# Operand rows 32 bytes further apart, second weight buffers 16 bytes later, in a float32r transformer chain on one core

## What is computed

```
hn = rmsnorm(h, norm_mix[0]);  q, k, v = split(hn @ w_qkv_a)
h  = h + stick_breaking(q, k, v) @ w_o_a
h  = h + (silu(n(h) @ w_gate) * (n(h) @ w_up)) @ w_down
...                              # layer two: rope, dilated attention, SwiGLU
mod = silu(c) @ w_ada + b_ada;   proj = modulated(h) @ w_in
y_a = (b * conv3(c_s * v_s)) @ w_short_out
y_b = silu(layer_norm(conv31(v_c * sigmoid(gl)) + b)) @ w_conf_out
x  = x + g1 * ((g_a * y_a + g_b * y_b) @ w_o);  x = x + g2 * swiglu(...)
```

## Time and profile before

| what | value |
|---|---|
| median of 2 runs | 2050.95 us (2049.29 to 2052.61) |
| profiled execution, first to last instruction | 2050.8 us |
| mean granted TensorE clock | 0.997 of full speed |
| PE (matmul) busy | 98% of the span |
| PEld (weight load) busy | 80% |
| DVE, ACT, POOL busy | 52%, 39%, 31% |

### The profile page before, as it was taken

How to read it: one execution, slowest core, us unless ns; L and a number is a source line. 1 busy time by engine, 2 the same in 40 slices (tenths; PEclk the granted TensorE clock), 3 DMA queues, 4 the chain that set the end, 5 groups by cost and what they waited for, 6 DMA issues and landing times.

```text
span 2050.8 us, 28727 instructions
## 1 busy us (share of the span) xinstructions
PE 2016.6 (98%) x9556; PEld 1645.1 (80%) x9556; DVE 1066.4 (52%) x1445; ACT 798.3 (39%) x1182; POOL 629.0 (31%) x416
## 2 busy tenths in 40 slices
PE   7999999999999999999999999999999999999997
PEld 5777788888887777788888888888888888888886
DVE  6666644343465666544343456699855552332324
ACT  5545443342253444454332354222227352222224
POOL 1111255341134333246341254444444031001013
PEclk9999999999999999999999999999999999999999
DMA  4122244443234344244443332233323323333333
GB/s 155 62 72 82 83 143 166 162 144 102 92 112 93 82 84 111 77 140 174 151 146 99 95 123 73 94 101 92 102 92 93 102 83 99 95 95 100 92 102 103
DMA packets 64036, 218.80 MB, mean 107 GB/s; under 512 B 7792, under 2 KB 9968, under 8 KB 63856
## 3 DMA queue, kind: packets, MB, share of 16 engines
q1 hardware_dynamic: 60912, 213.96, 32.8%
q0 software_dynamic: 3072, 4.20, 1.6%
HBM read 211.83 MB, written 2.10 MB: 104 GB/s over the span
## 4 chain that ended last, share of the span: by engine, by line
PE 92%; DVE 3%; issue 2%; ACT 1%; POOL 1%; DMA 1%; DVEq 0%; SPq 0%; ACTq 0%; POOLq 0%
PE G L1524 28%; PE G L1526 28%; PE G L1525 28%; PE Z L1648 2%; PE O L1666 2%; PE Z L1629 2%; PE Z L1524 1%; PE Z L1526 1%; PE Z L1525 1%; DVE ez L940 0%; DVE sp L923 0%; DMA raw<-stream 0%; DVE Z L1053 0%; PE O L1675 0%; DMA qkv<-tmp 0%
## 5 line engine op out<-in xcount | busy, mean ns | idle before, releaser
L375 ACT ACTIVATE wh<-raw 128x1024 fp32r<-128x1024 f32 x338 | 358.5, 1061 | 970.0 <-PE G L1526 957.5
L1524 PE MATMUL G<-xh,wh 128*128 128x512 f32 (+1 forms) x1616 | 634.0, 392 | 10.3 <-DVE xl L835 9.5
L1525 PE MATMUL G<-xl,wh 128*128 128x512 f32 (+1 forms) x1616 | 626.9, 388 | 0.0
L1526 PE MATMUL G<-xh,wl 128*128 128x512 f32 (+1 forms) x1616 | 626.9, 388 | 0.0
L806 DVE TENSOR_TENSOR wl<-raw,wh 128x1024 fp32r<-128x1024 f32 x277 | 385.5, 1392 | 180.8 <-ACT wh L375 177.6
L1524 PEld LDWEIGHTS G<-xh,wh 128*128 128x128 f32 x1616 | 304.0, 188 | 82.8 <-issue 15.0
L1524 PE MATMUL G<-yh,wh 128*128 128x512 f32 x904 | 352.1, 389 | 3.8 <-POOL yl L1420 2.1
L1526 PEld LDWEIGHTS G<-xh,wl 128*128 128x128 f32 x1616 | 303.9, 188 | 63.3
L1525 PEld LDWEIGHTS G<-xl,wh 128*128 128x128 f32 x1616 | 304.2, 188 | 61.6 <-issue 1.0
L1526 PE MATMUL G<-yh,wl 128*128 128x512 f32 x904 | 350.6, 388 | 0.0
L1525 PE MATMUL G<-yl,wh 128*128 128x512 f32 x904 | 350.5, 388 | 0.0
(11 more groups left out here) (245 smaller groups left out, 1970.5 us busy)
## 6 DMA issues: line engine op xcount, KB each, us to landing
raw<-stream SPq DMA_DIRECT2D x340, 512.0 KB, 3.5
araw<-ada_w SPq DMA_DIRECT2D x48, 512.0 KB, 4.3
fraw<-stream SPq DMA_DIRECT2D x8, 512.0 KB, 4.7
qkv<-tmp POOLq DMA_DIRECT2D x64, 64.0 KB, 4.0
h<-x_t SPq DMA_DIRECT2D x8, 256.0 KB, 6.8
out_t<-h SPq DMA_DIRECT2D x16, 128.0 KB, 1.8
con<-const_d SPq DMA_DIRECT2D x1, 1344.0 KB, 10.3
cs<-c_row SPq DMA_DIRECT2D x1, 512.0 KB, 4.2
```

Source lines behind the costliest of these rows:

```text
L375: eng.activation(wh[s][:, :, :], raw[s][:, :, :], ACT.Copy).then_inc(w_hi, 1)
L1524: eng.matmul(total, hi[:, k, :], src_h[:, k, cols], start=k == 0, stop=False)
L1525: eng.matmul(total, hi[:, k, :], src_l[:, k, cols], start=False, stop=False)
L1526: mm = eng.matmul(total, lo[:, k, :], src_h[:, k, cols], start=False, stop=k == kt - 1)
```

## The change

Only declarations change: no instruction is added, removed or put elsewhere, and the sizes of what is read and written stay.

```
+ROW_APART, HALF_LAP, STEP = 8, 0, 4
...
-        xh, xl = sb("xh", [P, KD, SEQ], F32R), sb("xl", [P, KD, SEQ], F32R)
-        yh, yl = sb("yh", [P, KD, SEQ], F32R), sb("yl", [P, KD, SEQ], F32R)
+        def rows(name, width, apart, skip=0):
+            t = sb(name, [P, skip + KD * (width + apart)], F32R)
+            return t[:, skip:].rearrange("p (k s) -> p k s", k=KD)[:, :, 0:width]
+
+        xh, xl = rows("xh", SEQ, ROW_APART), rows("xl", SEQ, ROW_APART)
+        yh, yl = rows("yh", SEQ, ROW_APART, HALF_LAP), rows("yl", SEQ, ROW_APART, HALF_LAP)
         raw = [sb(f"raw{s}", [P, KD, P]) for s in range(2)]
-        wh = [sb(f"wh{s}", [P, KD, P], F32R) for s in range(2)]
-        wl = [sb(f"wl{s}", [P, KD, P], F32R) for s in range(2)]
+        wh = [rows(f"wh{s}", P, 0, STEP * s) for s in range(2)]
+        wl = [rows(f"wl{s}", P, 0, STEP * s) for s in range(2)]
```

## The result

| | before | after |
|---|---|---|
| median of the runs, us | 2050.95 (2049.29 to 2052.61), 2 runs | 2086.03 (2084.65 to 2087.41), 2 runs |
| ratio | 1 | **1.017**, 95% interval 1.014 to 1.020 |
| profiled span, us | 2050.8 | 2085.5 |
| mean granted clock | 0.997 | 0.997 |

What follows compares the result with a forecast made beforehand. PE, busy 98% of the span with near-gapless matmuls, was taken as the bound. 3/4 of 7,800 full-width matmuls at -6.7 ns, the rest 0, gave 5.0 ns each, 39 us: 2050.8 - 39 = 2012 us; range 1975 to 2082.

Steps and rivals of the forecast that it cites:

- the 3/4 unknown relations: Full-width matmuls brought to weight-to-row placements the trace does not show; priced at -6.7 ns each, 39 us in sum.
- half the surplus: Gain assumed for unknown placements: 6.7 ns of the 13.3 ns by which each full-width matmul distance exceeds streaming 512 columns.
- the 256-column row: Trace passages of 256-column matmuls: 120.0 ns with `wh`, 113.8 ns with `fwh` 64 bytes apart; 6.2 ns better.
- The bound on the upper side: Most that an unknown placement was taken to cost a full-width matmul, +6.7 ns, from the nearest trace rows.
- relation 0: Weights and rows at equal places, counted modulo 128 bytes; said to remain for 1/8 of all matmuls, price 0.
- the matmuls that were counted at 64 bytes: 1/8 of all matmuls, with weights and rows 64 bytes apart modulo 128; between -6.2 and +6.7 ns, taken as 0.
- The two rows at 512 columns: Trace passages 64 bytes apart: `fwh`, 12 distances of 233.3 ns, and `x2h`/`x2l`, 9 of 228.9; worse by 6.7 and 2.3 ns.
- The second argument: For the -6.7 ns price: a relation changing with each row cannot settle into one bad rhythm for a whole product.
- The ceiling: Most that changing addresses could gain over all full-width matmuls: 7,800 x 13.3 ns = 104 us, giving 1947 us.
- price 0: DVE, ACT and POOL work beside PE, none over 3% of the chain; no new wait expected, so no time added.
- the slower rival: Changed relations cost full-width matmuls +2.3 to +6.7 ns, a new rhythm every three matmuls; 2069 to 2103 us, chance 0.23.
- distances unlike from row to row: Sign from 1250 us on: full-width distances under 226 ns, returning after four rows, differing between s = 0 and 1.

Runs made afterwards that it cites:

- m3_map: Kernel of matmuls alone, 512 columns, rows and weights each started at 16 places 16 bytes apart, 256 pairs; even-start mean 44.6 cycles beyond the columns, floor 32.
- m2_shapes: Kernel of matmuls alone with other widths, types and pitches; at 64 bytes 48 cycles beyond the columns for 512 columns, 16 for 256; at relation 0, 32.
- m5_columns: Kernel of matmuls alone, 96 per relation, at 256 and 512 columns, even and odd starts; the 512-column list matched the map in 25 of 32 places.
- m4_low_parts: Kernel of matmuls alone: only low parts moved (32 to 53 cycles beyond the columns), then row pitches of 2048 plus 0 to 128 bytes, then starts in 4-byte steps.
- w64: Kernel before with one unused tensor ahead of the weights, putting them 64 bytes further: 2095.83 us, ratio 1.022, distance 233.3 ns.
- w192: Kernel before with one unused tensor ahead of the weights, putting them 192 bytes further: 2065.76 us, ratio 1.007, distance 228.9 ns.

## Why the prediction was wrong

**The step that failed** is the price of the 3/4 unknown relations. It was taken as -6.7 ns, "half the surplus", from the 256-column row as the nearest. By the map it is positive. Taken over all full-width matmuls the prediction had -5.0 ns and the trace has +5.2: 10.2 ns on 7,800 matmuls are 80 us, and they make the whole of the miss, 2012 against 2086. The bound on the upper side, +6.7 ns, held for the mean, but not for each relation: 96 bytes costs 18.3 cycles over the floor, 7.6 ns.

**A second step was wrong and small:** the relations were counted modulo 128 bytes. They repeat modulo 256 only, so 1/16 of the matmuls keep relation 0, not 1/8; the other 1/16 stands at 128 bytes and costs 13 to 16 cycles. Nor are the matmuls that were counted at 64 bytes free: half stand at 64 (16 cycles over the floor), half at 192 (5.3).

**Why the row was the wrong neighbour.** Two kinds of nearness were at hand: same relation at another width, or same width at another relation. The forecast took the first. m2_shapes and m5_columns show that width changes the list itself; 64 bytes is the best relation at 256 columns and a bad one at 512. The two rows at 512 columns were few, 12 and 9 distances, but they were of the kind that 7,800 matmuls are, and both said "dearer". Read alone they give +2.3 to +6.7 ns.

**The second argument, that a relation which changes with each row cannot settle into a bad rhythm,** has a mirror image that the prediction used only in its rival: it cannot settle into the good one either. The row pitches of m4_low_parts show it, 43 to 47 cycles for all eight, and 45.4 where the single relations give 38.5.

**The ceiling** of 104 us was arithmetic on the surplus over 213.3 ns. As a ceiling it was not false, but nothing reaches into it: 32 cycles was the least in each of the more than 500 combinations at 512 columns. Half of it was no sensible middle value, since the kernel already stood at the edge of what places can give.

**What held.** That the kernel is a string of matmuls, that only their distance matters, and that the count is 7,800 (96 more, from `fwh`, were left out): w64, w192 and the change itself all follow from count and distance, less the part in the attention stages that waits anyway. That the place of one stream against the other counts in passages without waits, though not its bounds: at 512 columns no place was under the kernel before, and the dearest in steps of 16 bytes cost 10 ns (56 cycles). That DVE, ACT, POOL, the loads and the waits stay (price 0). That `x2h` gives 0.8 us at most; it gave nothing, its matmuls went from 229.9 to 232.6 ns (610 to 842 us, waits left out), since by the declared sizes it came to stand 128 bytes from `wh0` modulo 256 (45 to 48 cycles), not at 0. And the slower rival, with its mechanism (a new rhythm every three matmuls, 226.6 ns the best of the relations at full width), its sign to look for (229 to 236 ns) and its price, 2069 to 2103: the result stands in its middle. Its mechanism is half of it, since w64 shows that one relation kept throughout costs 6.7 ns too. It had 0.23. What spoke for it was both measured exceptions at 512 columns, and what spoke against was one at another width; weighed by that, it should have been the forecast.

**Right only in appearance:** "distances unlike from row to row, and unlike for s = 0 and 1, would show the mechanism". They are, and they did show that places matter, but upward. A sign in the trace that shows a mechanism does not show its direction; the prediction should have named the direction in it.

**Not settled:** why float32r has a floor of 32 cycles, what in the chip makes the two lists, and what chooses between two rhythms of one relation.

## What to carry to other kernels

If float32r matmuls stand back to back, read their distance before touching their addresses: 226.7 ns at 512 columns is the best that any placement here gave, and from that value no placement tried here won anything. If the distance is 229 to 236 ns, one unused tensor of 64 to 256 bytes ahead of the weights is a test of one line, and is worth up to 2%. When the price of something unknown is taken from the nearest row, take the row of the same shape first, even if it has few matmuls; and keep row pitches that leave every row at the same place modulo 256 bytes (2048 and 512 here; other multiples were not tried) unless a measurement asks otherwise.

## What the runs showed of the hardware that was not expected

- **The distance of float32r matmuls depends on the addresses of weights and rows.** At 512 columns it is 32 to 56 cycles beyond the columns in steps of 16 bytes (m3_map), by the difference of the starts modulo 256 bytes and the absolute start modulo 32 bytes; in steps of 4 bytes, both streams together, up to 58.7 (m4_low_parts).
- **The surplus depends on the type.** In m2_shapes nine bf16 matmuls of 512 columns take 2.11 us from the first start to the last end:

```profile
539.67 2.11 PE L84 MATMUL G<-xb,wbf 128*128 128x512 bf16 x9
```

Less one duration of 0.38 us that is 8 distances of 216 ns, 6 cycles beyond the columns, against 32 at best in float32r. The Trainium skill, TensorE: Matmul & The Clock Gate, Back-to-back issue gap, gives about 216 ns for 512 columns as the gap of isolated matmuls, and about 131 ns for a stream of weight loads and matmuls. The bf16 loop here is such a stream and stands at 216; 131 is in no run here. The same loop in float32r gives 226.7. Plain float32 took 429.2 ns, 6 cycles beyond 1024. Both other types ran at one placement only, so whether addresses count for them is open.
- **Below some width float32r matmuls get no shorter.** At 192 and at 128 columns both stand 111.7 ns apart (m2_shapes). The 128-column weight load is the same in both and may be the limit; that is argued, not shown. 111.7 ns is 268 cycles, so with 32 cycles beyond the columns the two limits would meet near 236 columns, an estimate.
- **Rhythms close on multiples of 16 cycles.** One float32r matmul takes 544 cycles, the dear patterns 1648 for three or 1120 for two; the pair of products of the changed kernel takes 26,704 cycles (48 distances of 231.8 ns, averaged over ten pairs), 1669 x 16.
